# Attention with a diagonal of reciprocal denominators: P turned by a matmul, four buffers of P, chains one unit longer

## The reference

```
scores = q k^T / 8 + bias            # masked outside the window
m      = max(max(scores), sink)      # the sink is a learned logit; the causal heads have none
p      = exp(scores - m)
out    = (p / (sum(p) + exp(sink - m))) v
y      = concat(..., out) @ w_out
```

## Time and profile before

| | |
|---|---|
| time, median of 3 runs | 3507.47 us (3503.13 to 3511.55) |
| the profiled execution | 3517.96 us, its span 3516.2 us |
| mean granted PE clock | 0.959 of full speed |
| busy share of the span: PE, PEld, DVE, ACT, POOL | 92%, 75%, 51%, 34%, 47% |
| chain that ended last, by engine | PE 71%, DVE 15%, ACT 7%, issue 4%, DMA 2% |
| first attention | about 416 to 528.8 us |
| second attention, short heads | about 2256 to 2361 us |
| second attention, causal heads | about 2361 to 2554.3 us |

### The profile page before, as it was taken

One profiled execution on the slowest core, in us unless ns is written; L12 is line 12 of the kernel. 1 busy time (PEld: TensorE's weight loads), 2 busy tenths in 40 slices (PEclk: granted clock), 3 DMA queues, 4 the chain that ended last, 5 costly groups with the idle time before them and its releaser, 6 DMA issues.

```text
span 3516.2 us, 40420 instructions
## 1 busy us (share of the span) xinstructions
PE 3244.8 (92%) x15143; PEld 2633.6 (75%) x15143; DVE 1805.5 (51%) x2429; ACT 1213.0 (34%) x2329; POOL 1656.6 (47%) x1159
## 2 busy tenths in 40 slices
PE   6978889899999999999999999888898999999987
PEld 3865568677777787788887888866677788887875
DVE  6879662878885225655522131365526655532133
ACT  3135362444442113333412130265513334312132
POOL 3321116655557667644476642210056644476652
PEclk8989899999999999999999999998899999999998
DMA  5524414322324432223245234444242223245232
GB/s 189 117 99 137 122 49 174 126 90 72 123 75 147 185 122 78 85 78 126 72 161 209 96 124 138 150 109 120 60 165 67 86 78 126 72 161 211 104 125 86
DMA packets 286911, 414.58 MB, mean 118 GB/s; under 512 B 26536, under 2 KB 211051, under 8 KB 285589
## 3 DMA queue, kind: packets, MB, share of 16 engines
q1 hardware_dynamic: 218968, 240.41, 22.8%
q10 hardware_dynamic: 62812, 154.67, 11.6%
q0 software_dynamic: 4960, 17.22, 1.5%
HBM read 324.79 MB, written 93.75 MB: 119 GB/s over the span
## 4 chain that ended last, share of the span: by engine, by line
PE 71%; DVE 15%; ACT 7%; issue 4%; DMA 2%; ACTq 1%; POOL 1%; SPq 0%; DVEq 0%; POOLq 0%
PE PS L900 63%; PE PS L2361 4%; DVE pl_ab L2478 1%; DVE cset L1340 1%; DVE ss L1216 1%; DVE cset L1338 1%; DMA w_raw<-ffn_w_down 1%; DVE pt L769 1%; PE PS L836 1%; ACT ph_ab L2412 1%; PE PS L2344 1%; DVE h_lo L894 1%; ACT pr_ab L2399 1%; ACT act L743 1%; DVE cset L1452 1%
## 5 line engine op out<-in xcount | busy, mean ns | idle before, releaser
L1244 POOL TENSOR_TENSOR sl<-ss,sh 128x512 fp32r<-128x512 f32 x300 | 436.4, 1460 | 478.6 <-ACT sh L1231 477.4
L290 POOL TENSOR_TENSOR w_lo<-w_raw,w_hi 128x512 fp32r<-128x512 f32 x460 | 641.0, 1425 | 16.0
L286 POOL CAST w_hi<-w_raw 128x2048 fp32r<-128x2048 f32 x115 | 226.9, 1973 | 658.1 <-DMA w_raw<-w_in 200.3
L1452 DVE TENSOR_TENSOR cset<-cset,PS 128x512 f32<-128x512 f32 x360 | 236.3, 684 | 403.2 <-PE PS L900 355.7
L900 PE MATMUL PS<-h_hi,sh 128*128 128x512 f32 x960 | 378.8, 395 | 27.2 <-ACT cset L1390 25.3
L900 PE MATMUL PS<-h_lo,sh 128*128 128x512 f32 x960 | 376.3, 392 | 0.0
L900 PE MATMUL PS<-h_hi,sl 128*128 128x512 f32 x960 | 376.2, 392 | 0.0
L971 DVE TENSOR_TENSOR a_lo<-aT,a_hi 128x1024 fp32r<-128x1024 f32 x66 | 104.2, 1582 | 487.6 <-ACT a_hi L968 487.6
L900 PE MATMUL PS<-w_hi,a_hi 128*128 128x512 f32 x1056 | 329.3, 393 | 19.6 <-POOL w_lo L290 14.8
L1231 ACT ACTIVATE sh<-ss 128x512 fp32r<-128x512 f32 x285 | 180.1, 632 | 478.5 <-DVE ss L1216 478.2
L900 PE MATMUL PS<-w_lo,a_hi 128*128 128x512 f32 x1056 | 328.1, 392 | 0.0
(11 more groups left out here) (362 smaller groups left out, 6348.6 us busy)
## 6 DMA issues: line engine op xcount, KB each, us to landing
w_raw<-ffn_w_down SPq DMA_DIRECT2D x88, 512.0 KB, 4.2
sr<-ffn_w_gu SPq DMA_DIRECT2D x80, 512.0 KB, 5.1
ad<-cset ACTq DMA_DIRECT2D x66, 512.0 KB, 3.1
w_raw<-w_down SPq DMA_DIRECT2D x44, 512.0 KB, 4.3
xs<-px ACTq DMA_DIRECT2D x40, 512.0 KB, 2.6
sr<-w_up SPq DMA_DIRECT2D x40, 512.0 KB, 5.1
aT<-ad ACTq DMA_DIRECT2D x3, 5632.0 KB, 17.2
w_raw<-w_out SPq DMA_DIRECT2D x32, 512.0 KB, 4.4
```

The source lines that it names most:

```text
L286: e.tensor_copy(w_hi[b][:, 0:n], w_raw[b][:, 0:n]).then_inc(S("w_hi"), 1)
L290: op = e.tensor_tensor(w_lo[b][:, s], w_raw[b][:, s], w_hi[b][:, s].bitcast(F32), ALU.subtract)
L1244: e.tensor_tensor(s.lo[p][:], src, s.hi[p][:].bitcast(F32), ALU.subtract).then_inc(S("s_op"), 1)
L1452: e.tensor_tensor(out, out, PS[:, b, :], op).then_inc(S("s_ev"), 1)
```

## The change

P is no longer transposed and divided later: PE multiplies each 128x128 block of P by a diagonal matrix of the reciprocal denominators (`a.dg`), which turns and divides in one real float32 matmul. The diagonal is made for each unit by POOL (`diagonal`) from a reciprocal that DVE takes for each unit (`share`). The sink becomes one more column of `pr`, written by POOL (`sink_column`), so that the row sum of the exponential contains it. The spreads, their copies, the scaling and the sinks' exponentials go. `y_high` (ACT) and `y_low` (now DVE) read bank 6 directly, one head at a time; so v of the shared heads is loaded as two copies of its 64 columns, once for each key/value head.

There are 4 buffers of `pr` and 3 banks for turned chunks (4, 5, 7). PE turns unit m first and then does scores of m + 3; exps runs two units ahead of high, score three ahead of low_. POOL's six gated lows stand between the diagonals of units 1 to 6 and the next. The output projection's first three row tiles no longer wait for the last groups.

```diff
         def out_pe(e, p):
...
-            e.wait_ge(S("at_nrm"), 12 if p == 0 else 44)
+            done = 12 if p == 0 else 44
...
                     if m in (0, 3):
...
+                        e.wait_ge(S("at_yl"), done - 4 if m == 0 and grp == 0 else done - 1 + grp)
                     rows_chunk_pe(e, g, g % NBUF, from_tiles(2 * m, grp),
-                                  ("n_tmp", p * 8) if grp else None,
+                                  ("n_tmp", p * 8) if grp else ("at_yl", [done - 4, done - 4, done - 4, done]),
                                   m == 0, m == 3, p)
...
+                self.pr = [at(f"pr_{s.name}{i}", [P, w1], F32, o) for i, o in enumerate((*pr, scr, scr + 4 * KB))]
+                self.dg = [at(f"dg_{s.name}{i}", [P, P], F32, scr + 8 * KB + i * 512) for i in range(2)]
...
+        TURN_BANK = (4, 5, 7)
...
+            w = P // len(d.v_cols)
             for i in range(2):
...
+                for r, c in enumerate(d.v_cols):
+                    e.dma_start(a.v[d.v_ver % 2][i][:, :, r * w:(r + 1) * w].bitcast(F32), vd[i][:, :, c:c + w])\
+                     .then_inc(S(f"at_v{d.v_ver % 2}"), 16)
...
             def turn_p(m):
                 d, b, k0, k1, chunks = s.units[m]
-                e.wait_ge(S("at_exp"), n + m + 1)
+                e.wait_ge(S("at_dg"), n + m + 1)
                 for q, c0, c1 in chunks:
-                    wait(e, S("at_lo"), s.ch0 + q - 1)
+                    if q >= 3:
+                        e.wait_ge(S("at_lo"), s.ch0 + q - 2)
+                    elif q == 2 and s is att_bi:
+                        e.wait_ge(S("gl_s"), 3)
                     for k in range(c0, c1):
-                        mm = e.transpose(PS[:, 4 + q % 2, (k - c0) * P:(k - c0 + 1) * P],
-                                         a.pr[m % 3][:, (k - k0) * P:(k - k0 + 1) * P], ident[:])
+                        mm = e.matmul(PS[:, TURN_BANK[q % 3], (k - c0) * P:(k - c0 + 1) * P],
+                                      a.pr[m % 4][:, (k - k0) * P:(k - k0 + 1) * P], a.dg[m % 2][:], start=True, stop=True)
                     mm.then_inc(S("at_tr"), 1)
...
-            def spread(g):
...
                 scores(e, s, a, 1)
+                scores(e, s, a, 2)
             else:
+                e.wait_ge(S("gl_s"), 1)
+                scores(e, s, a, 2)
                 e.wait_ge(S("gl_s"), 2)
             for m in range(s.n):
-                if m + 2 < s.n and (m % 4 or m == 0):
-                    scores(e, s, a, m + 2)
                 if m % 4 or m == 0:
                     turn_p(m)
-                else:
-                    spread(m // 4 - 1)
+                if m + 3 < s.n and (m % 4 or m == 0):
+                    scores(e, s, a, m + 3)
                 if m % 4 == 3:
-                    if m + 3 < s.n:
-                        scores(e, s, a, m + 3)
+                    if m + 1 < s.n:
                         turn_p(m + 1)
+                    if m + 4 < s.n:
+                        scores(e, s, a, m + 4)
                     values(m // 4)
...
         def exps(e, s, a, m):
...
+            if d.sink is not None:
+                e.wait_ge(S("at_sk"), n + m + 1)
+                w += 1
+            x = a.pr[m % 4][:, 0:w]
...
-            def sinks(g):
...
-            def spread_out(g):
...
             def y_high(g):
                 d = s.units[4 * g][0]
-                e.wait_ge(S("at_nrm"), g_ + g + 1)
-                e.activation(HI(d.slot, g % 2), a.t[g // 4 % 2][:, g % 2, :], ACT.Copy)\
-                 .then_inc(S("at_yh"), 1)
+                e.wait_ge(S("at_pv"), g_ + g + 1)
+                r = slice(d.half * HD, (d.half + 1) * HD)
+                e.activation(HI(d.slot, g % 2)[r], PS[r, 6, :], ACT.Copy).then_inc(S("at_yh"), 1)
 
             if s is att_ab:
                 exps(e, s, a, 0)
+                exps(e, s, a, 1)
...
             for m in range(s.n):
                 g = m // 4
-                if m + 1 < s.n and (m or s is att_ab):
-                    exps(e, s, a, m + 1)
+                if m + 2 < s.n:
+                    exps(e, s, a, m + 2)
                 high(m)
                 if s is att_bi and 1 <= m < 7:
                     gated_act(e, m - 1)
-                if m % 4 == 0 and g:
-                    spread_out(g - 1)
-                if m % 4 == 2 and g and (g - 1) % 4 >= 2:
+                if m % 4 == 1 and g:
                     y_high(g - 1)
-                if m % 4 == 3:
-                    sinks(g)
...
-            def denom(g):
...
+            def share(m):
+                e.wait_ge(S("at_exp"), n + m + 1)
+                e.reciprocal(ast[:, RD, m % 8:m % 8 + 1], ast[:, DEN, m % 8:m % 8 + 1]).then_inc(S("at_rd"), 1)
...
-            def scale(g):
...
+            def y_low(g):
                 d = s.units[4 * g][0]
...
+                e.wait_ge(S("at_yh"), g_ + g + 1)
+                r = slice(d.half * HD, (d.half + 1) * HD)
+                e.tensor_tensor(LO(d.slot, g % 2)[r], PS[r, 6, :], HI(d.slot, g % 2)[r].bitcast(F32), ALU.subtract)\
+                 .then_inc(S("at_yl"), 1)
 
             score(0)
             score(1)
+            share(0)
             if s is att_bi:
                 gated_dve(e, 0)
                 gated_dve(e, 1)
+            score(2)
             for m in range(s.n):
-                if m + 2 < s.n:
-                    score(m + 2)
-                if m % 4 == 1 and m > 1:
-                    scale(m // 4 - 1)
+                if m + 1 < s.n:
+                    share(m + 1)
+                if m + 3 < s.n:
+                    score(m + 3)
+                if m % 4 == 2 and m > 2:
+                    y_low(m // 4 - 1)
                 low_(m)
...
         def att_pool(e, s, a):
 
-            if s is att_bi:
-                for q in range(6):
-                    gated_low_pool(e, q)
-            for g in range(s.n // 4):
...
+            def sink_column(m):
+                d, _, k0, k1, _ = s.units[m]
+                if d.sink is not None:
+                    e.wait_ge(S("at_s"), n + m + 1)
+                    e.tensor_copy(a.pr[m % 4][:, (k1 - k0) * P:(k1 - k0) * P + 1], nsk[:, d.sink:d.sink + 1]).then_inc(S("at_sk"), 1)
+
+            def diagonal(m):
+                e.wait_ge(S("at_rd"), n + m + 1)
+                if m >= 2:
+                    e.wait_ge(S("at_tr"), s.unit_end(m - 2))
+                e.tensor_scalar(a.dg[m % 2][:], ident[:], ast[:, RD, m % 8:m % 8 + 1], None, ALU.mult).then_inc(S("at_dg"), 1)
+
+            sink_column(0)
+            sink_column(1)
+            e.wait_ge(S("w_used"), (G_OUT2 if s.z else G_OUT1)[0])
+            for m in range(s.n):
+                diagonal(m)
+                if m + 2 < s.n:
+                    sink_column(m + 2)
+                if s is att_bi and 1 <= m < 7:
+                    gated_low_pool(e, m - 1)
```

More of the change, by code:

```diff
@@ L1062, in out_act @@
         def out_act(e, p):
-            e.wait_ge(S("at_yl"), 6 if p == 0 else 22)
+            e.wait_ge(S("at_yl"), 12 if p == 0 else 44)
             if p == 0:
@@ L2142, in build, with __init__ @@
         class Head:
-            def __init__(self, q_row, k_row, k_ver, v_col, v_ver, row, slot, half, tab, off, width, keys, sink):
-                self.q_row, self.k_row, self.k_ver, self.v_col, self.v_ver = q_row, k_row, k_ver, v_col, v_ver
-                self.row, self.slot, self.half, self.tab, self.off, self.width = row, slot, half, tab, off, width
+            def __init__(self, q_row, k_row, k_ver, v_cols, v_ver, slot, half, tab, off, width, keys, sink):
+                self.q_row, self.k_row, self.k_ver, self.v_cols, self.v_ver = q_row, k_row, k_ver, v_cols, v_ver
+                self.slot, self.half, self.tab, self.off, self.width = slot, half, tab, off, width
                 self.keys, self.sink = keys, sink
@@ L2363, in values @@
                 mm.then_inc(S("at_pv"), 1)
-            def spread(g):
-                e.wait_ge(S("at_rd"), g_ + g + 1)
-                wait(e, S("at_rc"), g_ + g)
-                for k in range(4):
-                    r = 4 * (g % 2) + k
-                    mm = e.transpose(PS[:, 7, k * P:(k + 1) * P], ast[:, RD, r:r + 1].to_broadcast([P, P]), ident[:])
-                mm.then_inc(S("at_r"), 1)
             if s is att_ab:
@@ L2514, in att_dve @@
                     tab_dve(e)
-                if m % 4 == 3:
-                    denom(m // 4)
-            scale(s.n // 4 - 1)
+            y_low(s.n // 4 - 1)
         def att_pool(e, s, a):
-            if s is att_bi:
-                for q in range(6):
-                    gated_low_pool(e, q)
-            for g in range(s.n // 4):
-                if g % 4 < 2:
-                    continue
-                d = s.units[4 * g][0]
-                e.wait_ge(S("at_yh"), s.h0 + (g // 4) * 2 + g % 2 + 1)
-                e.tensor_tensor(LO(d.slot, g % 2), a.t[g // 4 % 2][:, g % 2, :], HI(d.slot, g % 2).bitcast(F32), ALU.subtract).then_inc(S("at_yl"), 1)
+            n = s.h0 * TT
```

(4 more changed lines are left out.)

71 lines of the change are left out of this document (20 added, 51 removed).

## The result

| | median | runs |
|---|---|---|
| before | 3505.68 us | 4 (3503.13 to 3511.55) |
| after | 3585.72 us | 4 (3581.32 to 3590.19) |

The ratio is 1.0222, 95% interval 1.0205 to 1.0238: slower by 80 us, where the forecast had 38.5. The profiled execution of after took 3587.5 us, 3585.7 of it span.

What follows compares the result with a forecast made beforehand. In the attention stretches it took an engine chain, with VectorE's list between value blocks, as the bound. Terms 11 + 7 + 9 + 15 + 1 - 4.5 = 38.5 us raise the 3507.47 us median to 3546 us; range 3510 to 3585.

Steps and rivals of the forecast that it cites:

- the walked case: Whole kernel: the main forecast from hand-walked engine timelines, 3546 us, own range 3520 to 3575, chance 63%.
- Turned by a matmul, 0.244 us a block: Turning P on TensorE: an fp32 product is two instructions of 0.122 us; 540 blocks cost 75 us more of TensorE.
- the last rival: Turning P costs what a transposition costs, so the change is nearly free: -42, about 3505 us; chance 2%.
- Diagonal 0.35 us: GpSimd's 128x128 scaled identity for each unit: estimated at 0.35 us, with 0.2 and 0.6 as ends.
- Steady first attention +11: First attention's 10 groups after the start: 8.3 us a block against 7.17, +11 us; ends -2 and +18.
- short heads +7: Second attention's eight heads of 256 keys: period 6.7 us against 6.22, +7 us, from 0 to +14.
- causal +9: Second attention's eight causal heads: 24.5 us a head against 23.4, +9 us, from -19 to +25.
- Start of the first attention +15: Gated lows between GpSimd's diagonals form a 3.8 us ring per unit; second block at 459.3 against 444.28, +15 us.
- The clock in the causal heads: Causal heads: real matmuls would hold TensorE at the full 2.4 GHz; a sag as before would add 12 us.
- clock sags: Rival: TensorE starved in the rings loses clock; causal heads +12, start +7, others +5: 3570 us; chance 10%.
- Ends -4.5: Ends of both attentions: the output projection no longer waits for spread, copy, scale; -4.5 us, or -2 without cover.
- The deeper look-ahead as a rival: More buffers, banks and scores ahead let TensorE run at its own sum in both attentions: -31, 3476 us; chance 10%.

Runs made afterwards that it cites:

- The identity: Changed kernel with P multiplied by the identity, no diagonals made, division left out: 3512.89 us, ratio to before 1.0013.
- the old order: Kernel before with its transpositions of P replaced by fp32 matmuls by the identity: 3508.61 us, ratio to before 0.9992.
- the scores first: Changed kernel with TensorE computing the scores three units ahead before it turns a unit: 3509.10 us, ratio to before 0.9997.
- the last run: Changed kernel with scores ahead of the turn, P turned by transposition, diagonals and waits kept, division left out: 3502.47 us, ratio to before 0.9995.
- all three edits: Changed kernel with scores ahead of the turn, gated lows behind diagonals of units 4 to 9, reciprocals one unit earlier: 3486.31 us, ratio to before 0.9940.
- the block-first experiment: Changed kernel with the block of values ahead of the next unit's turn and scores: 3634.10 us, ratio to before 1.0365.

## Why the prediction was right in sign and short in size

The measured 3585.7 us lies at the far end of the range, 3585, and outside the walked case's own 3520 to 3575. The prediction had stretched its range upwards for a sagging clock, and most of the loss beyond 38.5 us came from something else, more waiting in the steady groups. That the range reached this far is luck.

- *Turned by a matmul, 0.244 us a block: right.* Six instructions come 0.12 apart (0.83 us with the tail of the last), ten take 1.38 us. *That some 42 us of this price lie on the path* (what the last rival takes off the walks)*: wrong.* The identity gives 72.8 us back with the price kept, the old order hides it entirely, and with the scores first matmul and transposition are level.
- *Diagonal 0.35 us: too low.* It takes 0.605 (128 of them, below), just above the upper end of 0.6. The copy of the sink column, 0.186 us, was put at nothing ("where ScalarE has slack"), and exps does wait for it.

```profile
L2513 POOL TENSOR_SCALAR dg_ab<-ident,ast 128x128 f32<-128x128 f32 x128 | 77.5, 605 | 204.8 <-DVE ast L2469 202.4 <-PE PS L2348 1.3
L2507 POOL COPY pr_ab<-nsk 128x1 f32<-128x1 f32 x64 | 11.9, 186 | 41.3 <-DVE ast L2454 41.1
```

- *Steady first attention +11: +17.9 measured; short heads +7: +21.0; causal +9: +13.7.* This is the step that failed, 25.6 of the 31 us between 38.5 and 69.5. The walk "low(7) 5.80; the block starts at 5.93" let the block follow its own last low. In TensorE's list the block stands behind turn(8) and scores(11), and turn(8) needs a diagonal whose reciprocal VectorE takes only after low(6). And it let one score a group wait, for 0.73 us; two or three do, for 2.1 us in all in the first attention. The prediction's upper end for this stretch, +18, named such a case (a diagonal of 0.6 and waits on both scores); the short heads went past their end of +14. The periods were 9.6, 7.6 and 25.0 us (V17 to V31 over 7 heads: (2619.90 - 2445.06) / 7) against 8.3, 6.7 and 24.5. (For the causal heads the text has -19 as what TensorE alone would allow; (20.7 - 23.4) x 8 is -21.6, as in the rival.)
- *Start of the first attention +15: +21.2 measured*, the mechanism right (moving the lows gave 23.5 us). The size is the clause "with the turns at half clock it is +22": six instructions in 1.65 us, the half clock that transpositions had in the causal heads of before, in a stretch with a granted mean of 0.62.
- *The clock in the causal heads: right.* 0.99 against 0.89. The Trainium skill ("TensorE: Matmul & The Clock Gate", Part 4: PE-mode transpose) says that transpositions don't count as activity. The old order with real matmuls agrees (0.89 to 1.00), the last run limits it (1.00 with transpositions between the real matmuls). The rival "clock sags" held for the start; behind it the mean was 0.94 and 0.95 (before: 0.96 in both), and four of the blocks V1 to V11 of the first attention took 3.3 to 3.9 us instead of 2.2 (before: two, 4.2 us each).
- *Ends -4.5: right in kind, -2.8 and -3.6 measured*, from the last block's start to the first matmul of the output projection. 1.5 us of the second is not the wait that went but the block itself, 4.9 us in place of 6.37. The output projection starts with the block's end:

```profile
564.06 1.21 PE L2365 MATMUL PS<-ph_bi,vvl_bi 128*128 128x128 f32 x5
...
565.11 0.63 PE L900 MATMUL PS<-w_hi,h_hi 128*128 128x512 f32 x2
```

- *Start of the second attention +1:* V0 comes 2.7 us later behind its first scores.
- *The deeper look-ahead as a rival (3476 us, TensorE at its own sum, 20.7 us a head):* it failed for this change, and with TensorE's list reordered it is nearly what happens in the causal heads, 20.65 us from V15 to V31 (21.0 by the prediction's measure, V17 to V31 over 7). The prediction's exception ("only the causal heads could really gain") was right: with all three edits the first attention and the short heads are 1.2 and 2.2 us under before, the causal heads 16.1. The change carries a gain of 16 to 18 us there, and its order hides it.

What stays open: whether the sink columns behind the gated lows are all of the 7 us that the start keeps with the identity; what part of the last 3 us in the first attention (81.22 with the scores first against 77.96) is the copy of the sink column; and what lowers the clock. None was tried alone.

## What to carry to other kernels

On an engine that works in order, put what feeds the other engines (here the scores) ahead of what waits for a long ring (here the turn): the same instructions in the other order were 77 us apart. When a walk is made by hand, walk every list in its order up to the next repeat, and ask of each instruction what stands in front of it, not only what it waits for; the block's start was missed that way, and the block-first experiment too. A new operation in a mixed queue (the gated lows between the diagonals) ties two works that had nothing to do with each other, and so does a small one (the sink column) that is put there.

## What of the hardware was not expected

- The granted clock in the short heads fell to 0.66 with transpositions and late diagonals, 0.95 with matmuls in the same order and waits; with the scores ahead of the turn it was 1.00 in the causal heads with transpositions too, and 0.91 in the short heads.
- A 128x128 multiplication by a column took GpSimd 0.605 us, where the select on the same tile takes 0.29, half as much; a single column of one element a partition still takes 0.186 us.
